# Hybrid decoder layer: the first attention's product turned round (values as weights in two column halves) and both attentions in one loop

## The chip, the cores and the metric

One core of one Trainium2 chip. The time is the device time of one execution in microseconds (us); lower is better. Engines are named as in the profile: PE is TensorE (PEld its weight loads), DVE is VectorE, ACT is ScalarE, POOL is GpSimd, SP is SyncE, whose queue issues most DMAs.

## The reference, cut to what matters

One layer on x (512 tokens x 1024), in float32. RMSNorm and an input projection feed two mixers. The first (MLA) has 8 heads with queries and keys of 96 features and values of 64; the second (NSA) has 8 heads and three branches (selected blocks, window, compressed blocks), gated and added. Each mixer's output of 512 features is RMS-normalised over its features, both go through one output projection and are added to x; then RMSNorm and a squared-ReLU MLP.

```python
# MLA, per head: causal softmax, then the product with the values
p = masked_softmax(s, pos[None, :] <= qpos[:, None])      # exp(s - max) / sum
o = jnp.einsum('bhqk,bkhd->bqhd', p, v)
# join
mixed = concat([rms_norm(o_mla, grp_norm_mla), rms_norm(o_nsa, grp_norm_nsa)])
x = x + mixed @ w_o
```

## The kernel before

All matmuls keep float32 accuracy. Large projections split both operands into a high and a low part and add three products (`three`, lines 1444 to 1446); the attention products and the transposes use plain float32. A plain float32 matmul shows as two records in the profile, a transpose or a product of split parts as one.

The four blocks of 128 tokens are `t` = 0 to 3. The attention is a list of units (line 117): 32 MLA units (t, head), then NSA units `("sel", 3)`, `("win", 3)` and so on. Each engine has its program written out by hand, and each runs a loop over a step number n; the engines are tied by semaphores alone, each engine strictly in order:

- PE at step n: the scores of unit n (`score_unit`, L1629 for MLA, L1640 and L1641 for NSA), pieces of the NSA input projections (`project`), the product of unit n-4 (`mix_unit`, L1668), the transposes of the probabilities of unit n-2 (`turn_unit`, L1465), and other transposes.
- DVE at step n: `low_unit(n)` (L1110: add the mask or bias, row minimum), for even n the copy of the transposed probabilities of unit n-3 (`pt_out`, L1120), and inside the loop of step n norms of NSA keys and queries (`nsa_sum`, `nsa_row`, `nsa_turned`), low parts of weights (L949, L946) and `head_rows` of the last two rows of MLA keys.
- ACT: `exp_unit(n-1)` (L759, exp and its row sum), for odd n `pt_out(n-3)` (L769), high parts of weights, `pair_his`.
- POOL: `rotate` of the MLA heads (L527, L531), the power -1/2 of the norms (`rsqrt`, L473 and L476), small DMAs.

`mix_unit` of an MLA unit has the transposed probabilities (128 x 128 per block of keys) as weights and 64 columns of values moving; the result has tokens on partitions. After the 8 heads of a block `out_row` (L1131 to L1142, DVE) divides by the row sums into `o_mla`. Later, in the NSA part (u = n - 32), `mix_square` (L854, ACT) sums the squares, POOL scales the row into `mix_row` (L575), PE transposes it (`turn_mix(0, t)` at u = 9, 15, 20, 23) and ACT and DVE make its high and low part (`to_hi`, `mix_lows`, L963); `project_out(0, t, ...)` takes these from u = 28 on, and `residual` (L1350) adds the result to x.

MLA and NSA have a loop each on every engine. The first loop of PE ends with four steps without scores (`range(N_MLA + 4)`, L1677), then comes a wait (L1776) and the second loop. POOL waits for the last MLA product (L553) before it clears four tiles and issues 8 DMAs (L559) for the compressed branch, which PE needs at u = 7. SP loads x again (`X_AGAIN`, L449 to L452) once the block of weights before it is issued; x must be there for the first `residual`. A piece of `wo` is loaded right behind it and split at u = 20.

The table of position biases comes from four matmuls (`vec(i)`, L1542: 33 rows, 8 columns of weights, 512 or 112 moving columns) that stand after each of the four stages of the projection `ckv`, each with a copy by DVE (L997).

Of the kernel before, what the change touches and what calls it, by code (L numbers as in the profile page):

```python
# [20 lines left out]
F32 = mybir.dt.float32  # L21
# [107 lines left out]
MIXES = [(0, t) for t in range(NT)] + [(1, t) for t in reversed(range(NT))]  # L129
# [30 lines left out]
for _t in range(NT):  # L160
    NQ_BLOCKS[4 + _t] = [(2, _t), (3, _t)]

# [50 lines left out]
MIX_AT = {9: 0, 15: 1, 20: 2, 23: 3}  # L213
# [21 lines left out]
def build(nc, a, out, known):  # L235
    with ExitStack() as ctx:
# [14 lines left out]
        def signal(name, step=1):  # L251
# [25 lines left out]
        pt_buf = place("pt_buf", 2 * 512).rearrange("p (b n) -> p b n", b=2)  # L277
# [10 lines left out]
        stats = place("stats", 384)  # L288
# [3 lines left out]
        o_mla = place("o_mla", NT * 512, at=r_mla).rearrange("p (t n) -> p t n", t=NT)  # L292
# [30 lines left out]
        q_pairs = [place(f"q_pairs{i}", HEADS * P, F32R, at=r).rearrange("p (h s) -> p h s", h=HEADS)  # L323
                   for i, r in enumerate((r_mv + 4096, r_mla + 8192))]
        mix_row = place("mix_row", 2 * 512, at=r_mla + 12288).rearrange("p (b n) -> p b n", b=2)
# [21 lines left out]
        def stat(n):  # L347
            stat_at[0] += n
            assert stat_at[0] <= 384
            return stats[:, stat_at[0] - n:stat_at[0]]  # L350
# [9 lines left out]
        ones = stat(P)[0:1, :]  # L360

# [22 lines left out]
        probs, relu_done, a_hi_done = signal("probs"), signal("relu_done"), signal("a_hi_done")  # L384
        act_pt, exp_small = signal("act_pt"), signal("exp_small")
# [37 lines left out]

        def latent_bank(t):
            return (S + O)[t]
# [12 lines left out]
        def _(sp):  # L438
# [4 lines left out]
            for n, (what, i, width, split) in enumerate(PIECES):  # L443
# [22 lines left out]
        def _(pool):  # L466
# [69 lines left out]
            for i, key in enumerate(QK_ROWS):  # L536
                if i + 1 < len(QK_ROWS):
                    head_rsqrt(*QK_ROWS[i + 1])
                rotate(*key)

# [5 lines left out]
            for i, key in enumerate(NORMS):  # L546
                j = i % 2
# [3 lines left out]


            pool.wait_ge(*mixed.at(N_MLA - 1))  # L553
# [9 lines left out]
            def mix_row_of(g, t):  # L563
# [10 lines left out]
                src = o_mla[:, t, :] if g == 0 else o_nsa[:, t % 2, :]  # L574
                pool.tensor_scalar(mix_row[:, i % 2, :], src, rs_mix[:, at:at + 1], 1.0, ALU.mult, ALU.mult).then_inc(*mix_done.mark((g, t)))  # L575
# [10 lines left out]
            for t in range(3):  # L586
                mix_row_of(0, t)
            pool.wait_ge(*dve_step.at("kc_ss"))
            rsqrt("kc", kc_rs[0:64, :], kc_ss[0:64, :], HD)
            mix_row_of(0, 3)  # L590
# [20 lines left out]
        def _(act):  # L611
# [150 lines left out]
            def pt_out(n):  # L762
# [4 lines left out]
                if n >= 2:  # L767
                    act.wait_ge(*mixed.at(n - 2))
                act.activation(pt_buf[:, n % 2, 0:nk], TD[bank_of("T", ("p", n))][:, 0:nk], ACT.Copy).then_inc(*act_pt.mark(n))  # L769
# [9 lines left out]
            def norm_in(key):  # L779
# [3 lines left out]
                if i:  # L783
                    act.wait_ge(*summed.at(NORMS[i - 1]))
# [12 lines left out]
            def unit_step(n, last):  # L797

                if n - 3 >= 0 and (n - 3) % 2 == 0:
                    pt_out(n - 3)  # L800
                if n - 1 >= 0 and n - 1 < last:
                    exp_unit(n - 1)

            def pair_his(n):
# [10 lines left out]
                if n in PAIR_QUERIES:  # L815
                    t = PAIR_QUERIES[n]
                    dst = q_pairs[t % 2]
                    if n >= N_MLA:

                        act.wait_ge(*(mixed.at(N_MLA - 1) if t == 2 else scores.at(UNITS.index(("win", t + 2, HEADS - 1)))))  # L820
# [5 lines left out]
            for n in range(N_MLA):  # L826
                unit_step(n, N_MLA)
                pair_his(n)
# [9 lines left out]
                for m in SPLIT_AT_UNIT.get(n, ()):  # L838
                    split_hi(m)
# [9 lines left out]
            def mix_square(g, t):  # L849
                src = o_mla[:, t, :] if g == 0 else o_nsa[:, t % 2, :]  # L850
# [1068 lines left out]
```

## Time and profile before

| | us |
|---|---|
| median of 3 runs (lowest, highest) | 721.33 (717.14, 722.58) |
| the profiled execution's own time | 719.78 |
| its span in the profile | 718.0 |
| granted clock of PE, mean over the span | 0.988 |

The span is the time between the first and last instruction of the trace. "Idle before" in a row is the time for which that engine had nothing to do before the instruction, with what ended it behind the arrow. Ends of matmuls are modelled and overlap; the pace of PE is read from the distances of starts. Busy time of an engine counts overlapping records once.

### The profile page before, as it was taken

Reading aid. Unit: us, or ns where it says so; the run is one execution under the profiler, and the core shown is the slowest. Engines: PE = TensorE matmul, PEld = TensorE weight load, DVE = VectorE, ACT = ScalarE, POOL = GpSimd, SP = SyncE. Lnnn points to the kernel's source line nnn. Section 1 sums busy time; section 2 is a strip of 40 time slices with the busy share of each in tenths; the row PEclk is TensorE's granted clock in tenths of the full one; section 3 lists DMA queues with packets and bytes.
Section 4 is the critical chain, followed back from the end, with each engine's and each line's share of the span. In section 5 each row is a group of like instructions: output and inputs, shape, how many; then the busy total and the mean of one; then the engine's idle time right before and its main releaser. Section 6 shows DMA issues by size and latency. Waiting matters only on the chain.

```text
span 718.0 us, 9987 instructions
## 1 busy us (share of the span) xinstructions
PE 691.4 (96%) x3703; PEld 590.0 (82%) x3703; DVE 365.8 (51%) x716; ACT 294.8 (41%) x638; POOL 96.5 (13%) x148
## 2 busy tenths in 40 slices
PE   6999999999899999898899999999999999999998
PEld 4989778897789888687698888888888888888886
DVE  5645664788665865766745444423224444432311
ACT  5554664476565642646235433311212443321110
POOL 2526653221220201122000000000000000000000
PEclk9999999999899999899999999999999999999999
DMA  7331414200115100200033223223222322322302
GB/s 283 120 127 34 118 61 150 89 31 24 58 38 206 60 30 1 88 1 31 1 118 118 88 92 115 88 94 112 88 89 100 105 89 92 114 89 92 99 1 102
DMA packets 18386, 61.63 MB, mean 86 GB/s; under 512 B 2168, under 2 KB 2296, under 8 KB 18338
## 3 DMA queue, kind: packets, MB, share of 16 engines
q1 hardware_dynamic: 17138, 57.51, 23.9%
q0 software_dynamic: 1056, 3.42, 1.5%
q8 instruction: 30, 0.49, 0.3%
q14 instruction: 18, 0.15, 0.1%
q10 hardware_dynamic: 144, 0.07, 0.0%
HBM read 58.83 MB, written 2.15 MB: 85 GB/s over the span
## 4 chain that ended last, share of the span: by engine, by line
PE 84%; DVE 7%; ACT 3%; issue 3%; DMA 1%; POOL 0%; SPq 0%; DVEq 0%; ACTq 0%; POOLq 0%
PE bank L1444 14%; PE bank L1445 14%; PE bank L1446 14%; PE bank L1771 8%; PE bank L1770 8%; PE bank L1769 8%; PE bank L1465 5%; PE bank L1668 5%; PE bank L1710 1%; PE bank L1629 1%; DVE s_buf L1110 1%; PE bank L1640 1%; PE bank L1641 1%; DVE w_lo L946 1%; DMA x<-x 1%
## 5 line engine op out<-in xcount | busy, mean ns | idle before, releaser
L949 DVE TENSOR_TENSOR w_lo<-raw,w_hi 128x1024 fp32r<-128x1024 f32 (+3 forms) x89 | 103.4, 1167 | 119.5 <-ACT w_hi L625 119.4
L625 ACT ACTIVATE w_hi<-raw 128x1024 fp32r<-128x1024 f32 (+3 forms) x89 | 89.1, 1008 | 122.7 <-PE bank L1446 119.1
L1769 PE MATMUL bank<-act_hi,w_hi 128*128 128x512 f32 (+3 forms) x288 | 106.8, 371 | 0.0
L1771 PE MATMUL bank<-act_hi,w_lo 128*128 128x512 f32 (+3 forms) x288 | 106.7, 370 | 0.0
L1770 PE MATMUL bank<-act_lo,w_hi 128*128 128x512 f32 (+3 forms) x288 | 106.7, 370 | 0.0
L1444 PE MATMUL bank<-w_hi,a_hi 128*128 128x512 f32 x256 | 99.6, 389 | 0.0
L1445 PE MATMUL bank<-w_lo,a_hi 128*128 128x512 f32 x256 | 99.6, 389 | 0.0
L1446 PE MATMUL bank<-w_hi,a_lo 128*128 128x512 f32 x256 | 99.6, 389 | 0.0
L1444 PE MATMUL bank<-w_hi,act_hi 128*128 128x512 f32 (+3 forms) x224 | 90.2, 403 | 2.4 <-DVE act_lo L963 2.1
L1445 PE MATMUL bank<-w_lo,act_hi 128*128 128x512 f32 (+3 forms) x224 | 80.5, 360 | 0.0
L1446 PE MATMUL bank<-w_hi,act_lo 128*128 128x512 f32 (+3 forms) x224 | 80.5, 359 | 0.0
L759 ACT ACTIVATE p_buf<-s_buf,stats 128x128 f32<-128x128 f32 (+3 forms) x96 | 53.6, 559 | 49.8 <-PE bank L1465 28.3
L1409 DVE TENSOR_TENSOR sq_b<-relu_b 128x512 f32<-128x512 f32 x32 | 22.1, 692 | 82.0 <-ACT relu_b L928 82.0
L928 ACT ACTIVATE relu_b<-bank 128x512 f32<-128x512 f32 x32 | 19.1, 598 | 106.3 <-PE bank L1771 106.3
L1770 PEld LDWEIGHTS bank<-act_lo,w_hi 128*128 128x128 f32 x288 | 54.2, 188 | 9.2
L1769 PEld LDWEIGHTS bank<-act_hi,w_hi 128*128 128x128 f32 x288 | 54.2, 188 | 9.1
L1771 PEld LDWEIGHTS bank<-act_hi,w_lo 128*128 128x128 f32 x288 | 54.2, 188 | 8.9
L1444 PEld LDWEIGHTS bank<-w_hi,a_hi 128*128 128x128 f32 x256 | 48.1, 188 | 10.0
L1445 PEld LDWEIGHTS bank<-w_lo,a_hi 128*128 128x128 f32 x256 | 48.1, 188 | 9.9
L1446 PEld LDWEIGHTS bank<-w_hi,a_lo 128*128 128x128 f32 x256 | 48.1, 188 | 9.9
L1444 PEld LDWEIGHTS bank<-w_hi,act_hi 128*128 128x128 f32 x224 | 43.0, 192 | 11.1 <-DVE act_lo L963 3.1
L1668 PE MATMUL bank<-n_v,pt_buf 128*128 128x64 f32 x320 | 45.3, 273 | 4.2 <-ACT pt_buf L769 2.4
(193 smaller groups left out, 1072.3 us busy)
## 6 DMA issues: line engine op xcount, KB each, us to landing
raw<-weights SPq DMA_DIRECT2D x86, 512.0 KB, 3.3
x<-x SPq DMA_DIRECT2D x8, 512.0 KB, 6.3
raw<-weights SPq DMA_DIRECT2D x7, 384.0 KB, 4.3
bias<-bias_by_distance POOLq DMA_DIRECT2D x1, 2048.0 KB, 9.2
y<-x SPq DMA_DIRECT2D x8, 256.0 KB, 2.2
raw<-weights SPq DMA_DIRECT2D x4, 288.0 KB, 2.7
raw<-weights SPq DMA_DIRECT2D x4, 280.0 KB, 3.1
consts<-consts SPq DMA_DIRECT2D x1, 692.0 KB, 4.2
```

Of the source, the lines that this page charges most:

```text
L625: ins = act.activation(w_hi[:, m % RING, 0:width], raw[:, n % RAW, 0:width], ACT.Copy)
L759: act.activation(p_buf[:, n % 2, 0:nk], s_buf[:, n % 2, 0:nk], ACT.Exp, scale=-1.0, bias=neg_max[:, m:m + 1], accum_out=den[:, d:d + 1]).t ...
L949: ins = dve.tensor_tensor(w_lo[:, m % RING, 0:width], raw[:, n % RAW, 0:width], w_hi[:, m % RING, 0:width].bitcast(F32), ALU.subtract)
L1409: dve.tensor_tensor(sq_b[:, f % 2, :], relu_b[:, f % 2, :], relu_b[:, f % 2, :], ALU.mult).then_inc(*sq_done.mark((half, f)))
L1444: pe.matmul(dst, a_h, w_h, start=start, stop=False)
L1445: pe.matmul(dst, a_h, w_l, start=False, stop=False)
L1446: return pe.matmul(dst, a_l, w_h, start=False, stop=stop)
L1465: ins = pe.transpose(bank[0:m, i * step:i * step + k], tile, ident[0:k, 0:k])
L1668: ins = pe.matmul(bank[:, 64 * h:64 * h + 64], pt_buf[:, n % 2, j * P:(j + 1) * P], v, start=j == 0, stop=j == t)
L1769: pe.matmul(dst, h[:, ws], act_hi[:, k, cols], start=k == 0, stop=False)
L1770: pe.matmul(dst, h[:, ws], act_lo[:, k, cols], start=False, stop=False)
L1771: ins = pe.matmul(dst, l[:, ws], act_hi[:, k, cols], start=False, stop=k == KD - 1)
```

## The change

1. MLA products: `mix_pair` does two heads together. The values of a head (64 columns) are the weights, the transposed probabilities move (128 columns), and the two heads' results go to partitions 0 to 63 and 64 to 127 of the same columns of the bank. The result has features on partitions. The matmuls alternate between the two heads.
2. The probabilities must be divided before they are transposed: DVE takes the reciprocal of each unit's sum (`unit_den`), POOL multiplies (`weigh`), and `turn_unit` waits for that (`normed`).
3. The result needs no transposes for the output projection: ACT and DVE make high and low part right out of the bank (`ot_out`, `ot_low`). Squares are summed over the four feature groups by DVE and over partitions by one matmul with a column of ones (`ot_squares`); the norm's factor is applied in `residual` behind the projection.
4. One loop over all units on PE, ACT and DVE; POOL has a loop of 33 steps. POOL's clears and 8 DMAs wait for the last MLA scores instead of the last product.
5. Buffers: four transposed probabilities instead of two (two more places of 512 columns lie in x's space, `pt_far`), and one query pair lies there too. So the second load of x waits for the last MLA product and for the scores of `("win", 3, 7)` (u = 15) besides.
6. The four bias matmuls stand together, after the second stage of `ckv`, each in 8 rows at partition 0, 32, 64, 96 of two banks.

```diff
+            def weigh(n):
+                kind, t, h = UNITS[n]
+                p = p_buf[:, n % 2, 0:(t + 1) * P]
+                d = h + 8 * (out_of(n) % 4)
+                pool.wait_ge(*dve_step.at(("rden", n)))
+                pool.tensor_scalar(p, p, rden[:, d:d + 1], 1.0, ALU.mult, ALU.mult).then_inc(*normed.mark(n))
...
+            for n in range(N_MLA + 1):
+                if n - 1 in HEADS_AT:
+                    rotate(*HEADS_AT[n - 1])
+                if n >= 1:
+                    weigh(n - 1)
+                if n - 2 in NORM_AT:
+                    norm_rsqrt(NORM_AT[n - 2])
+                if n in OT_RS:
+                    ot_rsqrt(OT_RS[n])
...
-            pool.wait_ge(*mixed.at(N_MLA - 1))
+            pool.wait_ge(*scores.at(N_MLA - 1))
...
                 if n == X_AGAIN:
                     sp.wait_ge(*scaled.at(("nq", 0)))
+                    sp.wait_ge(*mixed.at(N_MLA - 1))
+                    sp.wait_ge(*scores.at(UNITS.index(("win", NT - 1, HEADS - 1))))
...
+            def ot_out(t):
+                n = HEADS * t + HEADS - 1
+                bank = O[t % 2].rearrange("p (c s) -> p c s", c=4)
+                act.wait_ge(*product_of(n))
+                act.activation(ot_hi[t], backwards(bank), ACT.Copy).then_inc(*ot_copied.mark(t))
...
+                act.activation(square, O[t % 2], ACT.Square).then_inc(*squares.mark(("mix", 0, t)))
...
+            def unit_den(n):
+                d = UNITS[n][2] + 8 * (out_of(n) % 4)
+                dve.wait_ge(*probs.at(n))
+                dve.reciprocal(rden[:, d:d + 1], den[:, d:d + 1]).then_inc(*dve_step.mark(("rden", n)))
+
+            def ot_low(t):
+                bank = O[t % 2].rearrange("p (c s) -> p c s", c=4)
+                dve.wait_ge(*ot_copied.at(t))
+                dve.tensor_tensor(ot_lo[t], backwards(bank), ot_hi[t].bitcast(F32), ALU.subtract).then_inc(*ot_rest.mark(t))
+                dve.wait_ge(*squares.at(("mix", 0, t)))
...
+                dve.tensor_reduce(ot_sum, by_token, AX.X, ALU.add).then_inc(*summed.mark(("mix", 0, t)))
...
-            for n in range(N_MLA, last + 9):
-                if n - 3 >= N_MLA and n - 3 < last and (n - 3) % 2 == 1:
+            for n in range(last + 9):
+                if n - 3 >= 0 and n - 3 < last and (n - 3) % 2 == 1:
                     pt_out(n - 3)
...
+                if n < N_MLA:
+                    mla_step(n)
+                if n >= 1 and n - 1 < N_MLA:
+                    unit_den(n - 1)
+                if n in OT_LO:
+                    ot_low(OT_LO[n])
...
+            def mix_pair(n):
+                _, t, h = UNITS[n]
+                pe.wait_ge(*act_pt.at(n))
+                pe.wait_ge(*dve_pt.at(n + 1))
...
+                for j in range(t + 1):
+                    for i in range(2):
+                        ins = pe.matmul(O[t % 2][64 * i:64 * i + 64, P * (h // 2):P * (h // 2) + P], m_v[:, j, (h + i) * VD:(h + i + 1) * VD],
+                                        pt_of(n + i)[:, j * P:(j + 1) * P], start=j == 0, stop=j == t)
+                ins.then_inc(*mixed.mark(n + 1))
+
+            def ot_squares(t):
+                pe.wait_ge(*summed.at(("mix", 0, t)))
+                pe.matmul(O[t % 2][:, 0:1], ot_sum, one_col, start=True, stop=True).then_inc(*turned.mark(("ss", t)))
...
-            for n in range(N_MLA + 4):
...
-                if n - 4 >= 0:
-                    mix_unit(n - 4)
...
-                if u in MIX_AT:
-                    turn_mix(0, MIX_AT[u])
...
-            for n in range(N_MLA, last + 10):
+            for n in range(last + 10):
...
+                if n - 4 >= 0 and n - 4 < N_MLA and (n - 4) % 2:
+                    mix_pair(n - 5)
```

## Rows read from the trace of the kernel before

**Rows 1.** The page: busy time of each engine, and the granted clock in 40 slices.
```profile
PE 691.4 (96%) x3703; PEld 590.0 (82%) x3703; DVE 365.8 (51%) x716; ACT 294.8 (41%) x638; POOL 96.5 (13%) x148
PEclk9999999999899999899999999999999999999999
```
**Rows 2.** Stretches: length, busy us of each engine (instructions), granted clock, DMA share, GB/s.
```profile
102.60:119.40 16.80, 15.55 (x88) 13.03 (x87) 10.24 (x30) 9.09 (x29) 7.94 (x9) 1.00 0.28 85
141.20:161.80 20.60, 20.60 (x151) 18.46 (x149) 17.53 (x47) 13.83 (x38) 5.16 (x6) 1.00 0.15 50
181.30:200.80 19.50, 16.27 (x96) 13.42 (x95) 13.35 (x34) 9.40 (x23) 5.31 (x13) 0.82 0.27 81
```
**Rows 3.** Timeline of PE from the last MLA scores on: start, duration, instructions, idle before.
```profile
181.30 1.02 PE L1629 MATMUL bank<-m_k,m_q 96*128 96x512 f32 x2
...
187.26 1.22 PE L1668 MATMUL bank<-m_v,pt_buf 128*128 128x64 f32 x8 [1.90 <-DVE pt_buf L1120]
...
192.41 0.77 PE L1640 MATMUL bank<-act_hi,q_pairs 128*128 128x512 f32 x1
...
200.82 0.47 PE L1640 MATMUL bank<-act_hi,q_pairs 128*128 128x512 f32 x1
```
**Rows 4.** PE's groups by line and shape: count | busy us, mean ns | idle before.
```profile
L1668 PE MATMUL bank<-m_v,pt_buf 128*128 128x64 f32 x160 | 23.2, 281 | 1.9 <-DVE pt_buf L1120 1.9
L1465 PE MATMUL bank<-consts,mix_row 128*128 128x128 f32 x32 | 4.9, 275 | 0.0
L1542 PE MATMUL bank<-onehot,consts 33*8 33x512 f32 x6 | 3.1, 590 | 0.0
```
**Rows 5.** Timeline of PE in one MLA unit of the last block.
```profile
177.01 1.02 PE L1629 MATMUL bank<-m_k,m_q 96*128 96x512 f32 x2
177.87 1.00 PE L1668 MATMUL bank<-m_v,pt_buf 128*128 128x64 f32 x8
178.71 0.61 PE L1465 MATMUL bank<-consts,p_buf 128*128 128x128 f32 x4
```
**Rows 6.** Weight loads by line and shape: count | busy us, mean ns | idle before.
```profile
L1769 PEld LDWEIGHTS bank<-act_hi,w_hi 128*128 128x128 f32 x288 | 54.2, 188 | 9.1
L1605 PEld LDWEIGHTS bank<-consts,hid_k 128*64 128x64 f32 x2 | 0.2, 134 | 0.2 <-issue 0.2
```
**Rows 7.** Timeline of PE around the first bias matmul.
```profile
35.60 0.29 PE L1446 MATMUL bank<-w_hi,act_lo 128*128 128x288 f32 x1
35.82 1.02 PE L1542 MATMUL bank<-onehot,consts 33*8 33x512 f32 x2
36.77 0.40 PE L1444 MATMUL bank<-w_hi,act_hi 128*128 128x288 f32 x1
37.01 0.29 PE L1445 MATMUL bank<-w_lo,act_hi 128*128 128x288 f32 x1
37.15 0.29 PE L1446 MATMUL bank<-w_hi,act_lo 128*128 128x288 f32 x1
```
**Rows 8.** DVE's reciprocal and POOL's scaling: count, duration ns min/median/max.
```profile
L1133 DVE RECIPROCAL stats<-stats x16: 202/203/204, 135.1 to 350.2; 128x8 f32<-128x8 f32 x16
L575 POOL TENSOR_SCALAR mix_row<-o_mla,stats x4: 692/696/701, 205.9 to 242.0; 128x512 f32<-128x512 f32 x4
```
**Rows 9.** Timelines of POOL, PE and DVE: the last rotations, a norm.
```profile
105.58 2.64 POOL L527 TENSOR_TENSOR rope_t<-qk_row,tab_k 128x128 f32<-128x128 f32 x2 [3.24 <-DVE qk_row L1062]
108.30 0.74 POOL L531 TENSOR_TENSOR qk_out<-qk_out,rope_t 128x256 f32<-128x256 f32 x1
...
109.16 0.27 PE L1465 MATMUL bank<-consts,p_buf 128*128 128x128 f32 x1
...
146.49 2.02 POOL L476 TENSOR_TENSOR stats<-stats 128x8 f32<-128x8 f32 x1
...
150.16 0.68 DVE L1178 TENSOR_TENSOR nq_row<-n_q,stats 128x512 f32<-128x512 f32 x1
```
**Rows 10.** The second load of x in SP's queue, and its last stretch (columns as rows 2).
```profile
217.26 1.91 SPq L452 DMA_DIRECT2D x<-x  x4
...
224.00:226.00 2.00, 2.00 (x15) 1.92 (x14) 1.72 (x6) 1.11 (x3) 0.00 (x0) 1.00 1.01 414
```

More of the change, by code:

```diff
@@ L360, in build @@
         ones = stat(P)[0:1, :]
+        one_col = stat(1)
         banks = [psum(f"bank{i}") for i in range(8)]
@@ L853, in mix_square @@
                     act.wait_ge(*squares.at(("mix", *MIXES[i - 1])))
-                act.activation(square, src, ACT.Square, accum_out=ss_mix[:, g * NT + t:g * NT + t + 1]).then_inc(*squares.mark(("mix", g, t)))
-            for n in range(N_MLA, N_MLA + 3):
-                if (n - 3) % 2 == 0:
-                    pt_out(n - 3)
-                if n - 1 < N_MLA:
-                    exp_unit(n - 1)
+                else:
+                    act.wait_ge(*summed.at(SQUARE_USERS[-1]))
+                act.activation(square, o_nsa[:, t % 2, :], ACT.Square, accum_out=ss_mix[:, g * NT + t:g * NT + t + 1]).then_inc(*squares.mark(("mix", g, t)))
             def ln_square(t):
@@ L1025, in _ @@
             latent_lo("cq", 1)
-            vec_out_of(1)
+            for j in range(4):
+                vec_out_of(j)
             split_lo(SPLITS[10])
@@ L1238, in _, with mla_step @@
             dve.wait_ge(*pool_step.at("gnq"))
[L1239 to L1243 removed]
+            def mla_step(n):
                 if n in HEADS_AT:
                     head_rows(*HEADS_AT[n])
[L1246 to L1247 removed]
                 if n - 5 in NORM_AT:
@@ L1536, in turn_latent, with vecs @@
                 turn((name, t), [c_row[:, t, lo + k * P:lo + (k + 1) * P] for k in range(n)], (turn_lo, (name, t)))
-            def vec(j):
-                lo, hi = 512 * j, min(512 * (j + 1), VEC)
-                bank = take("D", ("vec", j), (dve_step, f"vec{j}"))
-                known["bank", "T", ("vec", j)] = 2 + known["bank", "D", ("vec", j)]
-                pe.matmul(bank[0:8, 0:hi - lo], const("rel", 33), onehot[:, lo:hi], start=True, stop=True).then_inc(*turned.mark(("vec", j)))
+            def vecs():
+                pair = [take("D", ("vec", j), (dve_step, f"vec{j + 2}")) for j in range(2)]
+                for j in range(4):
+                    lo, hi = 512 * j, min(512 * (j + 1), VEC)
+                    known["bank", "T", ("vec", j)] = 2 + known["bank", "D", ("vec", j % 2)]
+                    ins = pe.matmul(pair[j % 2][32 * j:32 * j + 8, 0:hi - lo], const("rel", 33), onehot[:, lo:hi], start=True, stop=True)
+                ins.then_inc(*turned.mark("vec"))
             pe.wait_ge(*gain1_in.at())
@@ L1781, in _ @@
                     score_unit(n)
+                if n < N_MLA:
+                    for r, key in enumerate(ROWS):
+                        here = [i for i in range(4) if unit_of(r, i) == n]
+                        if here:
+                            project(*key, here)
+                if n in TURN_AT:
+                    turn_heads(*TURN_AT[n])
                 compress(n - N_MLA)
+                if n - 4 >= 0 and n - 4 < N_MLA and (n - 4) % 2:
+                    mix_pair(n - 5)
                 if n - 4 >= N_MLA and n - 4 < last:
                     mix_unit(n - 4)
-                if n - 2 >= N_MLA and n - 2 < last:
+                if n - 2 >= 0 and n - 2 < last:
                     turn_unit(n - 2)
+                if n - 4 in NORM_AT:
+                    turn_nsa(NORM_AT[n - 4])
+                if n in OT_SUM:
+                    ot_squares(OT_SUM[n])
                 if n - 9 >= N_MLA and n - 9 < last and UNITS[n - 9][0] == "cmp":
```

227 lines of the change are left out of this document (112 added, 115 removed).

## The prediction

> **What bounds the kernel now.** I read the page first: PE is busy for 691.4 of 718.0 us and its clock is full but for a few slices [rows 1]. So only PE time and the few holes of PE count; other engines matter where they make PE wait. Then I read stretches, to see which part is not simply PE at work. The stretch from the last MLA scores to the sixth NSA scores stands out: 19.5 us long, PE busy for 16.27, at a mean granted clock of 0.82, with DVE busy for only 13.35 [rows 2]. The timeline shows why: the first loop runs dry. PE waits 1.90 us for a copy of probabilities, its records grow longer, and the second loop starts from nothing at 192.41 [rows 3]. The opposite case is 141.2 to 161.8: PE never idle, but DVE busy for 17.53 of 20.60 us [rows 2]; work added to DVE there can show.
>
> **The pace of PE.** Two records of plain float32 with 512 moving columns take 177.87 - 177.01 = 0.86 us, so 128 columns take 107 ns. The eight records of a product with 64 moving columns and 128 columns of weights take 178.71 - 177.87 = 0.84 us, 105 ns each [rows 5]: twice their stream, so these wait for the weight loads. A load with 64 columns is 188 - 134 = 54 ns shorter than one with 128 [rows 6], so a load costs about 0.84 ns per column. Turning the product round thus swaps a 107 ns load with a 54 ns stream for a 54 ns load with a 107 ns stream. By itself that gains nothing: 107 ns a record either way. It gains only if the two column halves stream at once.
>
> **The parts.**
>
> (a) The products. 160 records [rows 4], or 17.1 us at 107 ns. The trace has no two column groups at work together, so I bound it. One end: the halves follow each other, 0 gained. Other end: each half's record overlaps one of the other. A float32 matmul has two records and the code alternates heads, so of 4(t+1) records a pair takes 2(t+1)+1 slots: 3, 5, 7, 9 for the four blocks, times 4 pairs, 96 slots or 10.3 us, 6.8 us less. I take the overlap, because a load's time by its columns shows that columns are filled apart and nothing that the halves write is shared; the other end stays a rival.
>
> (b) Going in and out of narrow columns. The bias matmul has 8 columns. After the record at 35.60 the next would start at 35.73 (the pitch is 0.14 in the last two rows); it starts at 35.82. Its 2 x 0.43 us would end at 36.68; the next starts at 36.77. That one is followed after 0.24 instead of 0.14 [rows 7]. Together 0.09 + 0.09 + 0.10, about 0.3 us. The load with 64 columns also has 0.2 us idle before it that nothing but issue explains [rows 6]. 16 pairs, once in and out each: +4.8 us. Bounds: 0 if loads for the halves can run ahead, 4.8 as in the row. I take 4.8, net with (a) -2.0.
>
> The page "TensorEngine Tiling (Array Packing)" of the Trainium skill, section Key Properties, says that tiles run independently but that changing the tiling mode drains the engine. The first half would give (a) its gain, the second is (b), and it speaks against a switch in each of 16 small pairs. The trace agrees with the drain (0.3 us); no row here shows the independence.
>
> (c) Removed: the transposes of the scaled MLA rows, 16 of 32 records [rows 4], 16 x 0.107 = -1.7 us, at places where PE is never idle. Added: four `ot_squares`, two records each with 128 columns of weights, +0.9 us. They wait for DVE's sum two steps before, which covers them.
>
> (d) Bias matmuls: 3 x 0.86 + 0.2 = 2.8 us of stream and four switches at 0.3, 3.9 us. Together they have one switch (3.1 us), and with overlap of column groups four slots of 0.43 (2.0 us). With (a)'s assumption -1.9, without it -0.9. DVE's four copies now come in one go; I count no wait of PE for them, since the weight piece that DVE splits behind them is for the projection after this one.
>
> (e) The joint loop. In the 19.5 us PE has: scores of one MLA unit 0.86 and five NSA units at 0.54, six products at 0.86, six times four transposes at 0.107, ten small ones and one switch, 12.6 us in all. So at most 6.9 us go. But DVE has 13.35 us of work there [rows 2], plus six reciprocals at 0.20 [rows 8], less `out_row` (1.1): 13.5 us, and it waits a little at each step. DVE becomes what is late next; I take 14.5 us, -5.0. Bounds: 0 if the chain score, minimum, exp, transpose, copy simply shows at each step, and 6.9.
>
> (f) The new wait. Between exp and transposes now lie DVE's reciprocal (0.20) and POOL's scaling (0.69 for 512 columns, less for fewer) [rows 8], and they stand in order behind other work. PE has two whole steps (4 to 6 us) between the scores and the transposes of a unit, so the bare chain is covered. Not covered are two places. First, POOL rotates the last heads ahead of `weigh(1)`: before, rotation ran from 105.58 to 109.04 and PE turned unit 1 at 109.16 [rows 9]. Now `weigh(0)` and its reciprocal, which stand behind `head_rows` on DVE, come ahead of the rotation, that begins about 1.5 us later, and `weigh(1)` comes behind it: PE waits about 1.2 us. Behind it on PE wait only scores, and the second rotation has a step of slack. Second, the power of a query norm (2.02 us on POOL, done at 148.5, used by DVE at 150.16 [rows 9]) now starts behind a `weigh` that itself waits for DVE's last instruction of a step; it ends about 1 us too late for DVE in the stretch where DVE is busy 17.5 of 20.6 us. Reciprocals add 0.20 per unit there (about 2.5 us over twelve units), and `ot_low` with its sum is 0.4 us dearer than `out_row`. I take +2.3 us for this stretch, +3.5 with the first place; bounds 0 and 7 (all of DVE's additions, 32 x 0.2, on the path).
>
> (g) In the NSA part DVE and ACT lose four pairs of conversions (0.7 us each) and two mix squares' worth of waits, where DVE made PE wait once for 1.1 us: -0.5. POOL's DMAs are issued earlier in steps; no cost.
>
> (h) The load of x. Before: from 217.26 to about 226.2 [rows 10]. It now starts at u = 15 instead of u = 11; with (e) that is about 220.5, done at 229.5, the piece of `wo` behind it at 231. Its split stands at u = 20, about 233. No cost, with 2 us to spare.
>
> **Sum.** (a) -6.8, (b) +4.8, (c) -0.8, (d) -1.9, (e) -5.0, (f) +3.5, (g) -0.5: -6.7 us. On the profiled execution's 719.78 that is 713.1. That execution lies 1.55 below the median of the three runs, so for a median I say 714.5. A measurement of this kernel tells about 1% (7.2 us) from no change, so the forecast sits on that line.
>
> **Rivals.**
>
> 1. The halves do not overlap: (a) is 0, (d) -0.9, the sum +1.1; but where DVE is late anyway the eight switches of blocks 2 and 3 (2.4 us) are hidden, so -1.3: 720.0. For it: in every row of the trace PE's records follow one another. Against it: disjoint columns and outputs.
> 2. The new wait is covered everywhere: (f) is 0 and (e) nearer its bound. 709.5. For it: two steps of slack. Against: DVE's 17.5 of 20.6 us.
> 3. Slower: DVE stands still in `unit_den` until ACT's exp is done, and with it the row minimum of the next unit, on which exp itself depends. So DVE and ACT, which work side by side now, take turns. If that costs 0.9 us per unit (exp of 512 columns 0.7 and the reciprocal 0.2) in the 16 units of blocks 2 and 3, it is +14.4 us instead of (f)'s 2.3: 726.5; on top of rival 1, 732. It decides the sign from 0.65 us per unit on. For it: DVE's load; against: exp(n-1) can start before the scores of n are out, while the reciprocal stands last in the step.
> 4. The load of x comes late (more gained before u = 15 doesn't help it, a slow transfer does): the split at u = 20 holds up ACT and PE by 2 to 3 us, 717.
>
> **How the numbers follow.** Forecast 0.48, rival 1 0.24, rival 2 0.12, rival 3 0.10, rival 4 0.06. Range: from rival 2 with a little more in (e), 708, to rival 1 with (f) somewhat dearer, 722. Half of the forecast case and all of rival 2 lie below 714.1 and a part of the others, 0.46 for faster; slower by over 1% is rival 3 and a tail of rival 1, 0.12; 0.42 for within 1%.
>
> **What would show it.** In the changed profile: pairs of block 3 on PE in about 1.0 us (overlap) or 1.7 (none), with 0.2 to 0.3 us at each entry and exit; 12.6 to 15 us from the last MLA scores to the sixth NSA scores, at full clock; PE idle ahead of L1465 for POOL's scaling near unit 1 and near units 19 to 23; DVE idle for the power. Wrong would be: idle of PE at every MLA step, a stretch of 19 us at the joint, or PE waiting for a weight piece near u = 20.

## The result, and the profile after

The changed kernel takes 722.77 us (median of 20 runs, 720.16 to 728.57), the kernel before 718.71 us beside it (20 runs, 715.33 to 722.58): ratio 1.005, 95% interval 1.0029 to 1.0071. The forecast was 714.5, with 722.0 as the upper end. The sign is wrong: a loss of about 3.6 us (0.5%) where a gain of 6.7 was summed. The forecast also stood on a median of three that lies 2.6 us above this one of twenty (721.33 and 718.71); counted from the later one it would have said 712.0.

The profile's page of the changed kernel, its busy times and its granted clock in 40 slices:

```profile
PE 686.3 (95%) x3695; PEld 579.6 (80%) x3695; DVE 369.6 (51%) x745; ACT 295.0 (41%) x634; POOL 112.0 (16%) x172
...
PEclk9999999999899999989999999999999999999999
```

Beside [rows 1]: PE has 5.1 us less to do, and yet the span is 721.1 us instead of 718.0. PE does less and stands more. The stretches say where. First the loop of the first attention, from its first scores to its last, in the kernel before (102.64 to 181.30) and then, in the second fence, in the changed one (99.85 to 187.35); behind it the stretch over the joint, to be read against the last of [rows 2]. Columns as in [rows 2].

```profile
102.64:181.30 78.66, 76.00 (x485) 64.93 (x483) 56.28 (x152) 47.46 (x133) 19.28 (x23) 1.00 0.23 76
```

```profile
99.85:187.35 87.50, 77.50 (x481) 58.72 (x480) 61.18 (x181) 52.09 (x142) 36.03 (x54) 0.98 0.20 68
187.35:204.49 17.14, 14.10 (x106) 11.11 (x105) 12.77 (x34) 8.68 (x22) 8.93 (x17) 0.80 0.31 91
172.00:174.00 2.00, 0.07 (x1) 0.00 (x0) 1.29 (x6) 1.55 (x5) 0.57 (x1) 1.00 0.00 0
174.00:176.00 2.00, 1.82 (x9) 1.82 (x10) 1.96 (x6) 0.67 (x2) 0.65 (x2) 0.55 0.01 4
```

The first scores come 2.79 us earlier (102.64 to 99.85): in the main the bias matmuls' gain (with them alone, e3 and e5 below, it is 1.92 and 1.65). The loop is 8.84 us longer, so the last scores come 6.05 us later. The joint stretch takes 2.38 us less (19.52 to 17.14), and the scores of the sixth NSA unit are 3.67 us late (200.82 to 204.49). From there on little changes: the profiled execution ends 3.1 us later. In the loop PE's idle time went from 2.66 to 10.0 us. The chain of waits names what PE waited for, from 97 to 200 (waits by line: engine, what for, us in total, times, longest):

```profile
POOL p_buf L593 <- DVE stats L1307: 50.7, 25, 4.9
ACT p_buf L818 <- PE bank L1534: 19.2, 12, 4.0
...
PE bank L1534 <- POOL p_buf L593: 10.5, 9, 3.0
DVE s_buf L1162 <- PE bank L1701: 9.2, 11, 2.6
```

L593 is `weigh`, L1307 the reciprocal in `unit_den`, L1534 the transposes, L818 the exp. The third row was not there before: nine waits of PE for the scaling, 10.5 us in all. ACT closes a ring: the exp of a unit waits for PE to have transposed the unit two before it (L818, 19.2 us, against 10.0 in the kernel before), since `p_buf` holds two. A late scaling so delays a transposition, and through it the next exp but one.

The longest of the nine can be followed instruction by instruction. Timeline of all engines from 187.49, cut to the chain:

```profile
187.49 0.68 DVE L1172 COPY pt_far<-bank 128x512 f32<-128x512 f32 x1
...
188.09 0.68 DVE L1162 CUSTOM_DVE_ANT_0 s_buf<-bank,consts 128x512 f32<-128x512 f32 x1
...
188.69 1.72 DVE L1275 TENSOR_TENSOR act_lo<-n_k,act_hi 64x256 fp32r<-64x256 f32 x4
188.81 0.72 ACT L818 ACTIVATE p_buf<-s_buf,stats 128x512 f32<-128x512 f32 x1 [0.67 <-DVE stats L1162]
...
190.44 0.16 DVE L1307 RECIPROCAL stats<-stats 128x1 f32<-128x1 f32 x1
190.52 1.40 DVE L999 SCALAR_TENSOR_TENSOR w_lo<-raw,consts,w_hi 128x512 fp32r<-128x512 f32 x2
190.70 1.69 POOL L593 TENSOR_SCALAR p_buf<-p_buf,stats 128x512 f32<-128x512 f32 x1 [3.90 <-DVE stats L1307]
...
192.45 1.12 PE L1534 MATMUL bank<-consts,p_buf 128*128 128x128 f32 x4 [3.04 <-POOL p_buf L593]
```

The exp and its sum are done at 189.63. The reciprocal starts at 190.44, because DVE is in its conversions (`pair_los`, L1275) until then. The scaling starts at once, but takes 1.69 us where it takes 0.69 elsewhere. PE resumes at 192.45, and its four transposes take 1.12 us instead of 0.66: half clock. Bare, exp, reciprocal and scaling are 1.7 us; here they take 3.6.

The steps that concern PE alone came out as forecast. Timeline of PE around a pair of block 3, and around the four bias matmuls (start, duration):

```profile
182.83 1.09 PE L1749 MATMUL bank<-pt_far,m_v 128*64 128x128 f32 x16
183.85 0.66 PE L1534 MATMUL bank<-consts,p_buf 128*128 128x128 f32 x4
...
38.91 1.03 PE L1613 MATMUL bank<-onehot,consts 33*8 33x512 f32 x8
39.88 0.87 PE L1534 MATMUL bank<-consts,c_row 128*128 128x128 f32 x6
```

16 records take 1.02 us from start to start, where two single units took 2 x 0.84 [rows 5]. The four bias matmuls take 0.97 us, where one took 0.95 [rows 7].

### The profile page after: what moved, and what is told of

Read it like the earlier page. It is cut to its first block, busy times and chain, and to the rows that moved or that the text cites. A ratio compares the mean times of both kernels' runs of the same rounds, so it can differ in the third digit from the quotient of the medians.

```text
span 721.1 us, 10028 instructions
## 1 busy us (share of the span) xinstructions
PE 686.3 (95%) x3695; PEld 579.6 (80%) x3695; DVE 369.6 (51%) x745; ACT 295.0 (41%) x634; POOL 112.0 (16%) x172
## 3 DMA queue, kind: packets, MB, share of 16 engines
HBM read 58.83 MB, written 2.15 MB: 85 GB/s over the span
## 4 chain that ended last, share of the span: by engine, by line
PE 82%; DVE 8%; ACT 4%; issue 3%; POOL 2%; DMA 0%; ACTq 0%; DVEq 0%; SPq 0%; POOLq 0%
PE bank L1513 14%; PE bank L1514 14%; PE bank L1515 14%; PE bank L1841 8%; PE bank L1840 8%; PE bank L1842 8%; PE bank L1534 6%; PE bank L1737 4%; PE bank L1781 1%; PE bank L1712 1%; PE bank L1713 1%; DVE w_lo L1002 1%; DVE s_buf L1162 1%; ACT p_buf L818 1%; PE bank L1701 1%
## 5 line engine op out<-in xcount | busy, mean ns | idle before, releaser
L1002 DVE TENSOR_TENSOR w_lo<-raw,w_hi 128x1024 fp32r<-128x1024 f32 (+3 forms) x89 | 103.4, 1166 | 120.4 <-ACT w_hi L684 120.3
L1513 PE MATMUL bank<-w_hi,act_hi 128*128 128x512 f32 (+3 forms) x192 | 77.1, 401 | 2.4 <-DVE act_lo L1016 2.2
L818 ACT ACTIVATE p_buf<-s_buf,stats 128x128 f32<-128x128 f32 (+3 forms) x96 | 53.6, 559 | 49.5 <-PE bank L1534 35.6
L1514 PE MATMUL bank<-w_lo,act_hi 128*128 128x512 f32 (+3 forms) x192 | 68.0, 354 | 0.0
L1515 PE MATMUL bank<-w_hi,act_lo 128*128 128x512 f32 (+3 forms) x192 | 67.9, 354 | 0.0
L1534 PE MATMUL bank<-consts,p_buf 128*128 128x128 f32 x248 | 47.4, 290 | 12.6 <-POOL p_buf L593 10.5
```

Source lines behind the costliest of these rows:

```text
L818: act.activation(p_buf[:, n % 2, 0:nk], s_buf[:, n % 2, 0:nk], ACT.Exp, scale=-1.0, bias=neg_max[:, m:m + 1], accum_out=den[:, d:d + 1]).t ...
L1002: ins = dve.tensor_tensor(w_lo[:, m % RING, 0:width], raw[:, n % RAW, 0:width], w_hi[:, m % RING, 0:width].bitcast(F32), ALU.subtract)
L1513: pe.matmul(dst, a_h, w_h, start=start, stop=False)
L1514: pe.matmul(dst, a_h, w_l, start=False, stop=False)
L1515: return pe.matmul(dst, a_l, w_h, start=False, stop=stop)
L1534: ins = pe.transpose(bank[0:m, i * step:i * step + k], tile, ident[0:k, 0:k])
```

## The experiments

Eleven kernels. Ratios are to the kernel before, with 95% intervals; its median beside them was 719.81 us (e1 to e4), 719.51 (e5 to e8) and 718.56 (e9 to e11). In e1, e7, e9, e10 and e11 `ot_low` also waits for ACT's square of the output instead of its copy; ACT makes the one right behind the other, and VectorE stands for the square in the first attention's loop only once, for 0.19 us in e9 and in e10.

### The scaling taken away (e1), and the reciprocal earlier (e2)

The changed kernel without `unit_den` and `weigh`; the probabilities stay unscaled, so the first attention's output lacks its division.

```
-                pe.wait_ge(*(normed if kind == "mla" else probs).at(n))
+                pe.wait_ge(*probs.at(n))
-                if n >= 1:
-                    weigh(n - 1)
-                if n >= 1 and n - 1 < N_MLA:
-                    unit_den(n - 1)
```

> The changed kernel without the scaling of the MLA probabilities: neither DVE's reciprocals nor POOL's 32 multiplications, PE transposes as soon as exp is done (so MLA's output is not divided by its sums). Theory A (the new wait is what ate the gain: PE's 10.5 us of waits for POOL, and the half clock behind the two long ones): about 12 us less than the changed kernel, 711 us, ratio to the kernel before 0.988. Theory B (DVE and ACT have too much work in the MLA steps, the wait is only where it shows): 2 to 4 us less, 719 to 721, ratio 1.00, and PE now waits as long for DVE or ACT.

Measured: 716.41 us, 0.9928 (0.9891 to 0.9965). So the scaling with its two hops costs 1.2 hundredths of the time, some 8.8 us (5.7 to 11.9 with both intervals), where the prediction's (f) had 3.5. That fits PE's 10.5 us of waits. The time lies between the two theories: most of A's 12 us comes.

e2 keeps everything and moves the reciprocal of unit n-1 right behind the row minimum of unit n:

```
                 if n < last:
                     low_unit(n)
+                if n >= 1 and n - 1 < N_MLA:
+                    unit_den(n - 1)
                 compress(n - N_MLA)
```

> The changed kernel with DVE's reciprocal of unit n-1 right behind the row minimum of unit n instead of last in the step; same work. Theory A: the wait comes from the place in DVE's queue, behind 1 to 3 us of norms, splits and key pairs; 5 us less, 718 us, ratio 0.998, POOL waits of PE halved or better. Theory B: no change within 1 us, 722. A third way: DVE now stands before an exp that isn't done and the norms behind it come late, 724.

Measured: 720.9 us, 1.003 (0.9989 to 1.0071), not told apart from the changed kernel. PE's waits in the profile (same view as above) say why:

```profile
PE bank L1534 <- DVE pt_far L1172: 3.7, 3, 1.5
PE bank L1534 <- POOL p_buf L593: 3.5, 5, 1.3
PE bank L1749 <- DVE pt_far L1172: 2.0, 1, 2.0
PE bank L1534 <- ACT pt_far L828: 1.3, 1, 1.3
```

The wait for the scaling falls from 10.5 to 3.5 us, and 7.0 us of waits for the copies behind the transposes stand in its place (0.5 in the changed kernel). DVE now stands for the exp (2.4 us in six waits for the probabilities, against 0.5 in one in the changed kernel) and is later with its copies. Theory A is right on the wait and wrong on the time: the place in DVE's queue is a trade, not a gain.

### The two parts that do not touch the products (e3, e4, e5)

e3 is the kernel before with the four bias matmuls together in two banks, e4 the kernel before with the joint loop alone, e5 with both. The core of each edit:

```
+                pair = [take("D", ("vec", j), (dve_step, f"vec{j + 2}")) for j in range(2)]
+                for j in range(4):
...
+                    ins = pe.matmul(pair[j % 2][32 * j:32 * j + 8, 0:hi - lo], const("rel", 33), onehot[:, lo:hi], start=True, stop=True)
```

```
-            for n in range(N_MLA, last + 10):
+            for n in range(last + 10):
...
-                if n - 4 >= N_MLA and n - 4 < last:
+                if n - 4 >= 0 and n - 4 < last:
                     mix_unit(n - 4)
```

> The kernel before with only the four bias matmuls put together in four groups of 8 columns. If the groups stream at once (as the start of the changed kernel's first scores, 2.8 us earlier, suggests): 2.8 us less, 716, ratio 0.996. If it is only three switches saved: 0.9 us less, ratio 0.999.

> The kernel before with only the joint loop (one loop on PE, ACT and DVE, POOL's clears and DMAs behind the last scores; products, transposes and norm as before). Theory A: the joint loop is worth what I forecast for it, about 5 us: 714, ratio 0.993. Theory B (DVE and ACT have no room at the joint): 1 to 2 us, ratio 0.998.

> The kernel before with the joint loop and with the four bias matmuls together, the first attention left as it was. Alone the two gave ratios 0.9918 and 0.9951. Theory A: they add, since they act in different stretches (the start of the first attention, and its end): ratio 0.987, 2 thousandths either way, near 710.5 us. With the changed kernel without its scaling at 0.9928 this would say that the turned products with all that hangs on them, scaling left out, cost 4 us instead of winning 8. Theory B: the early start given by the bias matmuls is eaten in the loop (VectorE is the later engine at its end), ratio 0.991 to 0.993 as the joint loop alone.

Measured: e3 715.97 us, 0.9951 (0.9917 to 0.9986); e4 712.91 us, 0.9918 (0.989 to 0.9946); e5 710.73 us, 0.9865 (0.9815 to 0.9915), theory A in each. The two add. In e3's profile the first scores stand at 100.72 instead of 102.64, 1.92 us earlier, as much as (d) had; what the ratio gives beyond that (3.5 us in all) lies within its interval. The joint, which this edit does not touch, took 17.11 us in that profile (179.36 to 196.47) instead of 19.52: PE waits 1.89 us there as before, but no spell at half clock follows. In e4's, the stretch from the last MLA scores to the scores of the sixth NSA unit is this row:

```profile
181.06:194.58 13.52, 12.70 (x96) 10.51 (x95) 12.20 (x31) 9.30 (x23) 5.32 (x13) 1.00 0.38 118
```

13.52 us against 19.50 in [rows 2], at full clock; PE's 12.70 us of work is the 12.6 that (e) counted. This stretch alone gives 6.0 us, and the timed gain is 5.9. By e3's row some 2.4 of the 6.0 are the half clock of the one profiled execution, and 3.6 are the loop. e5 beats both kernels and leaves nothing of the computation out.

The pair also closes the account of the changed kernel. e1 has everything that e5 has and the turned products besides, the division left out. It stands at 0.9928 against 0.9865: 4.5 us slower by the ratios, where PE's work alone would make it faster. The two intervals overlap, but each of e5's four executions (709.88 to 711.56 us) is shorter than each of e1's ten (712.78 to 719.30).

Where it goes can be read by stretches, between starts of PE's scores in each profile (us; single executions, those of the kernel before and of the changed one with a spell at half clock in the last stretch; e7 and e8 follow below):

| from, to | before | e5 | e1 | e7 | e8 | changed |
|---|---|---|---|---|---|---|
| first scores, unit 16 | 38.62 | 38.61 | 39.60 | 41.51 | 39.63 | 41.43 |
| unit 16, unit 24 | 20.57 | 20.57 | 21.11 | 21.61 | 22.43 | 23.62 |
| unit 24, last MLA scores | 19.47 | 19.48 | 18.24 | 21.08 | 23.90 | 22.45 |
| last MLA scores, sixth NSA scores | 19.52 | 13.51 | 15.66 | 15.75 | 14.98 | 17.14 |

The turned products without their division (e1 against e5) cost 0.99 and 0.54 us, gain 1.24 in the last block and cost 2.15 at the joint. The division (changed against e1) costs 1.83, 2.51, 4.21 and 1.48 us, 10.0 in all. The first 1.8 us come only where POOL scales ahead of and between its rotations (changed and e7), and not in e8, where DVE does it; e8 pays in the last block instead.

### The turned products (e6, e9)

e6 is the changed kernel with the heads of a pair one after the other, so that neighbouring matmuls share a column half:

```
-                for j in range(t + 1):
-                    for i in range(2):
+                for i in range(2):
+                    for j in range(t + 1):
```

> The changed kernel, with the two heads of a pair one after the other instead of record by record in turn: the same matmuls, no two neighbours on different column halves. Theory A: taking turns is what lets them overlap; without it a pair of block 3 goes from 1.02 us to about 1.7, the 16 pairs cost some 5.4 us more on TensorE, and in a loop where TensorE is busy nine tenths of the time 2 to 5 us of that show: ratio to the kernel before 1.008 to 1.012. Theory B: the time saved in the pairs is only waited away in front of the next transposes, for GpSimd: pair 1.7 us, but the same kernel time as the changed kernel, 1.003 to 1.007. Theory C: the weight loads alone set the pair, it stays near 1.0 us and nothing changes.

Measured: 724.29 us, 1.0038 (1.0009 to 1.0067), the same as the changed kernel's 1.005. A pair of block 3 in its profile:

```profile
195.54 1.58 PE L1749 MATMUL bank<-pt_far,m_v 128*64 128x128 f32 x16
197.05 0.65 PE L1534 MATMUL bank<-consts,p_buf 128*128 128x128 f32 x4
```

1.51 us instead of 1.02. In block 2 a pair takes 1.07 instead of 0.81 us, in blocks 1 and 0 the order changes almost nothing (0.60 against 0.58, 0.37 in both). So taking turns gives a part of the overlap, and a growing one with the block, not all of it; over 16 pairs e6 asks PE for 3.1 us more, not for theory A's 5.4. None of the 3.1 shows in the ratio, and its intervals leave room for less than 2 us; between executions of the same mean granted clock (0.986 to 0.993) e6's spans are 0.6 to 2.2 us longer. So theory A is out and B holds in the main: at most a part of the overlap is worth time here. It was tried only in the kernel with the division, where PE waits for the scaling.

Where do the 4.5 us between e5 and e1 come from? Up to the scores at 179 they are level: the loop takes 78.66 us in e5 (100.99 to 179.65) and 78.95 in e1 (100.16 to 179.11). Then e1's timeline of PE shows a hole, and DVE's what lies in front of it:

```profile
179.11 1.02 PE L1697 MATMUL bank<-m_k,m_q 96*128 96x512 f32 x2
182.50 1.59 PE L1745 MATMUL bank<-pt_far,m_v 128*64 128x128 f32 x16 [2.37 <-DVE pt_far L1170]
```

```profile
179.75 0.18 DVE L1260 TENSOR_SCALAR gates<-gates 128x24 f32<-128x24 f32 x1 [2.34 <-ACT gates L834]
179.97 0.30 DVE L1262 RECIPROCAL gates<-gates 128x24 f32<-128x24 f32 x1
180.19 0.63 DVE L1311 TENSOR_TENSOR ot_lo<-bank,ot_hi 128x512 fp32r<-128x512 f32 x1
180.73 1.03 DVE L1316 TENSOR_REDUCE ot_sum<-square 128x128 f32<-128x512 f32 x1
181.68 0.68 DVE L1170 COPY pt_far<-bank 128x512 f32<-128x512 f32 x1
```

DVE has nothing to do for 2.34 us, waits for the gates, then does 1.5 us on the turned output, and only then the copy that PE needs. e9 takes the output's two operations ahead of the gates' row (in e1, so again without the division):

```
                 pair_los(n)
+                if n in OT_LO:
+                    ot_low(OT_LO[n])
                 if n < N_MLA:
                     mla_step(n)
```

> The changed kernel without the scaling (as e1), and in it the low part and the sum of squares of the turned output taken on VectorE ahead of the gates' row instead of behind it. In e1 TensorE stood 2.37 us at 180 to 182.5 for VectorE's copy of the last pair; in front of that copy VectorE waited for the gates until 179.75 with nothing to do from 177.4, and then did the 1.5 us of these two first. Theory A: this order makes the hole: the copy comes 1.5 us earlier, the hole falls to 1 us, the 5 us at half clock behind it do not come, and the kernel gains 2 to 4 us on e1: ratio 0.986 to 0.990. Theory B: the hole is the gates' wait and VectorE's load as a whole, the time moves elsewhere: ratio as e1, 0.991 to 0.995.

Measured: 713.48 us, 0.9917 (0.9885 to 0.9949); by the ratio 0.8 us less than e1, and inside theory B's bounds. In the profile theory A's chain is there: the wait fell from 2.37 to 0.83 us, and the spell at half clock behind it is gone. The stretch 182 to 186 in e1, then in e9:

```profile
182.00:186.00 4.00, 3.50 (x24) 3.10 (x25) 3.93 (x10) 1.08 (x3) 3.52 (x8) 0.62 0.43 127
```

```profile
182.00:186.00 4.00, 2.96 (x29) 2.35 (x26) 3.93 (x11) 1.83 (x5) 4.00 (x9) 1.00 0.43 105
```

What the ratio leaves of this is small. Profiles of single executions differ by such spells (last section), so the 4.2 us between the two profiled spans (715.0 and 710.8) are no measure of the edit. e9 is 3.7 us behind e5 by the ratios, with intervals that overlap, and yet in the profiled executions the two are level at the scores of unit 61 (251.27 and 251.25). The executions' mean granted clocks go with the difference: at 0.995 e9's spans are 708.8 and 708.9 us, e5's 708.1, 708.1 and 709.7, but three of e9's six executions stand at 0.986 to 0.988 (712.4 to 714.7), and none of e5's four is under 0.993. e1 has six of ten at 0.981 to 0.986 (714.4 to 717.4), and at 0.993 it is about 1 us behind e5 (710.4 and 710.9 against 709.7). So most of the 4.5 us between e1 and e5 comes with executions in which the clock falls more; why it falls more often with the turned products was not tested. PE's waits from 97 to 200 are 7.5 us in e9 and 3.9 in e5; two thirds of the surplus are waits for copies of probabilities (3.5 us in e9 and 1.1 in e5). It was not tried to issue products in pairs without turning them.

### Other ways to divide (e7, e8, e10, e11)

e7 gives the reciprocal to POOL as well; e8 gives the scaling to DVE; e10 is e7 with e9's order on DVE; e11 is the changed kernel with that order alone.

```
-                pool.wait_ge(*dve_step.at(("rden", n)))
+                pool.wait_ge(*probs.at(n))
+                pool.tensor_tensor(rden[:, d:d + 1], den[:, d:d + 1], neg_one, ALU.pow).then_inc(*pool_step.mark(("rden", n)))
+                pool.wait_ge(*pool_step.at(("rden", n)))
```

```
                 dve.reciprocal(rden[:, d:d + 1], den[:, d:d + 1]).then_inc(*dve_step.mark(("rden", n)))
+                dve.wait_ge(*dve_step.at(("rden", n)))
+                dve.tensor_scalar(p, p, rden[:, d:d + 1], 1.0, ALU.mult, ALU.mult).then_inc(*normed.mark(n))
```

> The changed kernel, where GpSimd takes the reciprocal itself (a power of -1) instead of waiting for VectorE's. Theory A: a good part of the price lies in the hop over VectorE, whose reciprocal stands behind copies, splits and low parts in its queue: without it the scaling starts right after the exp, TensorE's waits for GpSimd fall from 10.5 us to under 6, and 3 to 5 us come back: ratio to before 0.998 to 1.002. Theory B: the price is GpSimd's own time for the scaling, 0.4 to 1.7 us of one unit: the power adds another 0.2 us or so to each, the waits stay at 10 us or grow, ratio 1.003 to 1.010.

> The changed kernel, where VectorE does the scaling itself right behind its reciprocal; GpSimd does nothing for it. VectorE is busy 72.0 us of the 103 from 97 to 200 and gets some 32 times 0.3 us more. Theory A: what costs is GpSimd's slow scaling (1.3 to 1.7 us where VectorE is busy beside it) and the hop: the chain gets shorter, ratio to before 0.995 to 1.000. Theory B: VectorE is the engine that decides in this loop, and every 0.3 us given to it shows as on the rival of the prediction that has it stand in the reciprocal: slower than the changed kernel, 1.008 to 1.015.

> The changed kernel with two repairs that keep its result: GpSimd takes the reciprocal itself (e7, 1.0007) and VectorE takes the turned output's parts ahead of the gates' row. Theory A: the two act at different waits and add; the second gives 1.5 us and perhaps a spell at half clock: ratio 0.996 to 0.999. Theory B: GpSimd's chain is the later one at the end of the loop anyway, nothing comes: 0.999 to 1.002. It stays behind the joint loop with the bias matmuls (e5, 0.9865) in both.

> The changed kernel, scaling and reciprocal as they are, with only VectorE's two operations on the turned output ahead of the gates' row. Theory A: TensorE's waits for the scaling decide there and VectorE's reciprocal of that unit stands behind the gates, so nothing is gained: ratio as the changed kernel, 1.003 to 1.007. Theory B: the 1.5 us show here too: 1.000 to 1.003.

Measured: e7 719.9 us, 1.0007 (0.9978 to 1.0037); e8 723.33 us, 1.0031 (0.9994 to 1.0069); e10 716.97 us, 0.9984 (0.9954 to 1.0015); e11 723.73 us, 1.0046 (1.001 to 1.0082). In e7 the power costs POOL 0.61 us each time, four times DVE's 0.15, and the chain is still shorter. PE's largest waits in e7:

```profile
PE bank L1536 <- DVE pt_far L1176: 2.7, 2, 1.4
PE bank L1536 <- POOL p_buf L597: 2.4, 3, 1.6
PE bank L1751 <- DVE pt_far L1176: 1.9, 1, 1.9
```

and in e8, from 97 to 200:

```profile
PE bank L1535 <- DVE p_buf L1308: 7.4, 6, 1.9
PE bank L1702 <- DVE stats L1160: 1.1, 1, 1.1
```

Read together: with the reciprocal on POOL, the wait for the scaling falls from 10.5 to 2.4 us. With reciprocal and scaling both on DVE it stays at 7.4, though POOL is out of the chain. So the wait for the scaling hangs on the turn in DVE's queue more than on POOL's arithmetic. Not so in the first 16 units: there, by the table above, moving the reciprocal (e7) changes nothing, and moving the scaling to DVE (e8) saves the 1.8 us. That is theory A of e7, in the wait and in the ratio. By the ratios e7 wins back 3.1 us of 8.8 (its interval and the changed kernel's overlap a little); the rest comes back as waits for DVE's copies, as in e2. e8 landed between its two theories and tells by its waits only. e11 gave nothing, as its theory A said; e10 against e7 is 1.7 us by the ratio, within the intervals, but its interval lies wholly below the changed kernel's. e10 is the best form of the turned attention that divides, and level with the kernel before; e5 is 8.6 us ahead of it by the ratios.

## Why the prediction was wrong

**(a), (b), PE's own cost: right.** From start to start a pair takes 0.37, 0.58, 0.81 and 1.02 us by block in the changed kernel, where two single units took 0.34, 0.78, 1.22 and 1.68 (e5; block 3 in [rows 5]). Over 4 pairs of each block that is 5.0 us less (6.8 forecast). Entry and exit cost 0.09 and some 0.05 us, 2.2 over 16 pairs (4.8 forecast): the last row before a pair takes 0.32 instead of 0.23. The net is -2.8 against -2.0, close because both terms were too large, which is luck. Rival 1 falls: the halves overlap. The page "TensorEngine Tiling (Array Packing)" of the Trainium skill, section Key Properties, was cited for both, tiles that run independently and a drain at each change of the mode; the trace agrees with the first (four bias matmuls in 0.97 us) and with the second at some 0.14 us for in and out, under half of the 0.3 taken from [rows 7]. (c) was right but for a size: two `ot_squares` take 0.29 us in the loop, so four 0.6, not 0.9.

**(d) and (e): right.** e3's first scores come 1.92 us earlier (-1.9). The joint loop alone gives 5.9 us by the ratio (-5.0), and its stretch is 13.5 us. Some of that is clock, which the term did not price: at the same mean granted clock (0.995 and 0.999) e4's spans are 3.3 to 3.8 us under those of the kernel before. DVE did not become later than PE there, as (e) feared: without the new attention its 12.20 us fit beside PE's 12.70.

**(f), the failed step.** It said: "PE has two whole steps (4 to 6 us) between the scores and the transposes of a unit, so the bare chain is covered. Not covered are two places." The bare chain is covered; the chain that runs is not bare. Each hop stands in the order of its queue: the reciprocal behind splits, conversions and the gates' wait on DVE, the scaling behind a power or beside a DVE split on POOL. One hop late is waited for by the next. The named places did show: waits of 0.55 and 0.64 us at 105.35 and 107.92, and up to the scores of unit 16 the division costs 1.83 us (1.2 forecast); from there to the scores of unit 24 (141.28 to 164.90) it costs 2.51 (2.3 forecast), where PE waits for the scaling (2.5 us in three waits). But from there to the last scores it costs 4.21 us, with waits of 2.10 and 1.48 us (at 174.18 and 186.85), and over the joint, where one wait is 3.04 us, another 1.48. These were priced at nothing. The bound of 7 for (f) was "all of DVE's additions on the path", 32 x 0.2: it counted durations and not the time that an instruction stands in a queue. e1 gives 8.8 us by the ratio, above that bound (its lower end, 5.7, is not).

**The sum of (a) to (c), the second failure.** It booked PE's saving as time. In a loop where PE, DVE and ACT hand each unit on, it was not: e6 changes a pair of block 3 by 0.49 us, and the kernel time moves by less than 2 us, if at all. The new attention without its division is 4.5 us slower than the old one (e1 and e5), instead of 2.8 faster. In the profiles, up to the sixth NSA scores, 2.4 of these 4.5 stand in the stretches (a spell at half clock among them); there a pair waits for both copies, and the output's low part and sum stand in front of one of them, which by e9's ratio is worth 0.8. The rest goes with executions of a lower granted clock, and its cause stays open. The prediction saw that `ot_low` is dearer than `out_row`, and priced it at 0.4 us of DVE's time, not by who waits behind it.

**(h) and the rivals.** (h) was right: PE waited for no weight piece in the changed kernel, and rival 4 falls with it. (g) had -0.5: from the scores of the sixth NSA unit to those of unit 61 the changed kernel gains 0.27 us. Rival 3 had the sign, but not the mechanism: DVE stood only 0.5 us in `unit_den`; the others waited for it. With the reciprocal moved forward (e2) that standing began, 2.4 us, far below its 14.4. (By its own terms the sign turns at (6.7 + 2.3)/16 = 0.56 us per unit, not 0.65.) Rival 2 is what e1 measures, the wait gone: 716.4, not 709.5, because of the second failure. The account by ratios: bias matmuls -3.5, joint loop -5.9, together -9.7 (e5); turned products without division +4.5; division +8.8; sum +3.6 (each step is the difference of two ratios, so the sum fits by construction, and each has 2 to 5 us of room).

## What to carry to other kernels

A new link in a chain between engines is priced by what stands in front of it in each queue and by who waits behind it, not by its duration; two steps of slack are used up by two hops that each wait out one long neighbour. Work taken from the busiest engine is time only while the others keep up: before booking it, change it in one cheap variant, as e6 does. When a change has several parts, run the ones that touch no dependency alone: here two of them hold the whole gain, 1.35%.

## What the runs showed of the hardware

**Column groups of TensorE overlap fully.** Four matmuls of 8 columns each in four groups take 0.97 us in the changed kernel, one took 0.95 before. Two halves of 64 columns, taken in turns, take 1.02 us for 16 records, 64 ns each, where 128 columns stream in 107 ns. Whether loads or streams hold them can't be told here: 16 loads take 0.87 us (54 ns each), and 16 streams of 107 ns, two at a time, would take 0.86. One head after the other the same 16 records take 1.51 us, 94 ns each, which is still under 107.

**A scaling on GpSimd stands while VectorE runs a split.** `weigh` on 512 columns takes 0.69 us, six times of eight; twice it takes 1.69 and 1.70. Both times it starts inside a split of weights on VectorE with two inputs in SBUF (w_lo, L999, here at 190.52 for 1.40 us) and ends 0.5 us after it. The same holds for 384 columns once (1.58 instead of 0.59, beside L999) and for 128 columns at 103.89 (1.41 instead of 0.37, beside L1002); every scaling that took longer than its kind ran beside a split. Beside VectorE's copies out of PSUM and its row minimum it keeps its 0.69. The rotation shows the same with the neighbour taken away. Its two products, in e1 and then in the changed kernel:

```profile
103.10 2.63 POOL L562 TENSOR_TENSOR rope_t<-qk_row,tab_k 128x128 f32<-128x128 f32 x2 [2.29 <-DVE qk_row L1112]
```

```profile
105.27 0.87 POOL L562 TENSOR_TENSOR rope_t<-qk_row,tab_k 128x128 f32<-128x128 f32 x2
```

In e1 VectorE multiplies (L1120, 103.05 for 0.96 us) and splits (L1000, 104.13 for 1.28) beside them, both with two inputs in SBUF; in the changed kernel the split has ended at 105.14. That the two engines share a way to SBUF is a reading of these rows.

**The clock can fall behind a hole.** In the changed kernel PE is idle for 2.10 us before 174.18, and the granted clock is 0.55 in the 2 us from 174, near the lower level of 1.2 GHz. The kernel before and e3 have the same wait at the joint, 1.90 and 1.89 us; behind it the clock is 0.50 from 189 to 193 in the one and 1.00 in the other. In e1 it is 0.62 after the wait of 2.37 us, and in e9, where that wait is 0.83 us, 1.00. So not every hole is followed by a spell: waits of 1.29 and 0.80 us (at 249.12 and 250.53) stand in the changed kernel, with the clock at 1.00 up to 256, and in e1 this follows the same two (at 239.40 and 240.80):

```profile
240.00:250.00 10.00, 9.21 (x42) 8.75 (x42) 6.32 (x20) 5.44 (x14) 0.00 (x0) 0.55 0.13 48
```

A hole that is closed so gives more than its length in one execution and nothing in another. That is why ratios over many runs were used for the verdicts here, and profiles only for where the time stood.
